# The second expert table's tiles loaded two at a time into neighbouring buffers

## The reference

```python
idx, gates                      # 8 heads x 16 picks per token, out of 128 x 128 experts
pre = einsum('tkd,td->tk', expert_u[idx], x)
act = gelu(pre) * gates
out = einsum('tk,tkd->td', act, expert_v[idx])
```

## Time and profile before

| | us |
|---|---|
| median of 3 runs | 2081.62 |
| lowest, highest run | 2081.34, 2082.43 |
| the profiled execution's own time | 2077.09 |
| its span | 2075.2 |

### The profile page before, as it was taken

One profiled execution on the slowest core, in us unless ns is written; L12 is line 12 of the kernel. 1 busy time (PEld: TensorE's weight loads), 2 busy tenths in 40 slices (PEclk: granted clock), 3 DMA queues, 4 the chain that ended last, 5 costly groups with the idle time before them and its releaser, 6 DMA issues.

```text
span 2075.2 us, 38095 instructions
## 1 busy us (share of the span) xinstructions
PE 2031.3 (98%) x12186; PEld 1857.8 (90%) x12186; DVE 1631.0 (79%) x2517; ACT 1092.8 (53%) x1460; POOL 719.6 (35%) x422
## 2 busy tenths in 40 slices
PE   7999999989999999999999999999999999999997
PEld 6888778988789999999999999999999899999876
DVE  7885777974667888888888656989898888888856
ACT  6543566454435745545554544555555555555554
POOL 0030200000001878888788860233232323334000
PEclk9999999999999999999999999999999999999999
DMA  5755558225555887788788877899999889999554
GB/s 207 257 182 182 173 172 296 110 92 193 192 173 178 212 210 206 209 209 207 210 208 207 218 243 245 319 353 357 340 360 335 297 309 324 369 339 334 201 185 150
DMA packets 172084, 496.14 MB, mean 239 GB/s; under 512 B 48720, under 2 KB 49008, under 8 KB 170352
## 3 DMA queue, kind: packets, MB, share of 16 engines
q1 hardware_dynamic: 117344, 413.39, 58.9%
q0 software_dynamic: 51200, 67.25, 12.6%
q10 hardware_dynamic: 3472, 14.72, 1.9%
HBM read 476.24 MB, written 19.04 MB: 239 GB/s over the span
## 4 chain that ended last, share of the span: by engine, by line
PE 90%; DVE 5%; DMA 2%; DVEq 1%; ACT 1%; issue 1%; ACTq 0%; SPq 0%
PE ps L263 27%; PE ps L2046 19%; PE ps L268 15%; PE ps L2051 10%; PE ps L289 5%; PE ps L283 5%; PE ps L284 5%; DVE lo L243 1%; DMA raw<-in_expert_v 1%; DVE act_pair L369 1%; PE ps L1914 1%; PE ps L1924 1%; DMA raw<-in_w_in_cols 0%; ACT hi L237 0%; PE ps L2012 0%
## 5 line engine op out<-in xcount | busy, mean ns | idle before, releaser
L237 ACT ACTIVATE hi<-raw 128x1024 fp32r<-128x1024 f32 x724 | 768.0, 1061 | 853.9 <-PE ps L263 385.1
L243 DVE TENSOR_TENSOR lo<-raw,hi 128x1024 fp32r<-128x1024 f32 x724 | 890.3, 1233 | 346.1 <-ACT hi L237 316.3
L1721 POOL DMA_INDIRECT gate_map<-gate_in_sb x256 | 471.2, 1841 | 537.7 <-DVEq L1473 462.1
L263 PE MATMUL ps<-act_pair,hi 128*128 128x448 f32 (+1 forms) x2816 | 656.6, 375 | 0.8 <-DVE act_pair L369 0.7
L263 PEld LDWEIGHTS ps<-act_pair,hi 128*128 128x128 f32 x2816 | 504.5, 189 | 53.3 <-DVE act_pair L369 3.4
L268 PEld LDWEIGHTS ps<-act_pair,lo 128*128 128x128 f32 x2816 | 371.8, 191 | 19.9 <-DVE lo L243 5.0
L268 PE MATMUL ps<-act_pair,lo 128*128 128x224 f32 (+1 forms) x2816 | 375.5, 276 | 2.6 <-DVE lo L243 2.6
L2046 PE MATMUL ps<-stage,hi 128*128 128x448 f32 x1024 | 231.9, 367 | 1.9 <-DVE gate_in_sb L1575 0.8
L2046 PE MATMUL ps<-act_pair,hi 128*128 128x448 f32 x1024 | 229.6, 366 | 1.1 <-ACT hi L237 1.1
L1738 POOL DMA_INDIRECT arena<-in_u_table,few_pick x64 | 103.0, 1610 | 305.7 <-DVE keep L1523 268.9
L2046 PEld LDWEIGHTS ps<-stage,hi 128*128 128x128 f32 x1024 | 183.1, 189 | 16.4 <-DVE gate_in_sb L1575 2.3
(11 more groups left out here) (287 smaller groups left out, 1663.6 us busy)
## 6 DMA issues: line engine op xcount, KB each, us to landing
raw<-in_expert_u SPq DMA_DIRECT2D x256, 512.0 KB
raw<-in_expert_v SPq DMA_DIRECT2D x256, 512.0 KB
raw<-in_w_in_cols SPq DMA_DIRECT2D x64, 512.0 KB
raw<-in_w_in_rows SPq DMA_DIRECT2D x48, 512.0 KB
raw<-in_w_out SPq DMA_DIRECT2D x32, 512.0 KB
raw<-in_w_pq SPq DMA_DIRECT2D x32, 512.0 KB
raw<-in_w_gate SPq DMA_DIRECT2D x32, 512.0 KB
gate_map<-stage SPq DMA_DIRECT2D x1, 14336.0 KB, 41.2
```

Of the source, the lines that this page charges most:

```text
L237: act.activation(hi[:, use, :], raw[:, slot, :], ACT.Copy).then_inc(hi_ready, 1)
L243: dve.tensor_tensor(lo[:, use, :], raw[:, slot, :], hi[:, use, :].bitcast(F32), ALU.subtract).then_inc(lo_ready, 1)
L263: mm = pe.matmul(first_tokens(out_ap), hi[:, use, d8 * P:(d8 + 1) * P], first_tokens(act_pair[:, d, :]), start=(d == 0), stop=False)
L1721: pool.indirect_dma_start(gate_map, bass.IndirectOffsetOnAxis(ap=place[0:n, unit, r:r + 1], axis=0), gates_out[0:n, unit, r:r + 1], None, ...
```

## The change

The table's layout in HBM is changed on the host: two chunks that follow each other lie side by side in a row, so that a pair of tiles is 128 rows of 8 KB. `value_block` issues two DMAs of 1 MB in place of four of 512 KB, each into two neighbouring buffers of `raw`. The wait before each is that for the pair's second tile: tile n - 3 subtracted, n being the pair's first. The completion is counted on the semaphore of the even slot alone. ScalarE's `round_tile` waits for that semaphore for both tiles of a pair; for the tiles behind the stage, `tile_at` takes off the 64 turns that the odd slots' semaphores have not counted. Rounding, subtraction, multiplication and their order are unchanged.

```diff
--- before.py
+++ after.py
@@ -229,8 +229,8 @@
                 sp.wait_ge(lo_ready, n - RAW + 1)
             sp.dma_start(raw[:, slot, :], src).then_inc(weights_landed[slot], 16)
 
-        def round_tile(act, n, slot, use, turn, first=False):
-            act.wait_ge(weights_landed[slot], 16 * turn + 16)
+        def round_tile(act, n, slot, use, turn, first=False, pairs=False):
+            act.wait_ge(weights_landed[slot // 2 * 2 if pairs else slot], 16 * turn + 16)
             if not first:
                 act.wait_ge(hi_used, n - SPLIT + 1)
                 act.wait_ge(lo_ready, n - SPLIT + 1)
@@ -246,8 +246,9 @@
         def tile_at(base, i, per, k):
 
             assert base % RAW == 0 and per % RAW == 0
+            unlanded = 2 * CHUNKS // RAW if base >= T_PLE and k % 2 == 1 else 0
             return (base + k + per * i, (base + k) % RAW, (base + k) % SPLIT,
-                    (base + k) // RAW + (per // RAW) * i)
+                    (base + k) // RAW + (per // RAW) * i - unlanded)
 
 
         def pair_tile(pe, n, use, k, out_ap, turn=None, tokens=SEQ):
@@ -582,9 +583,12 @@
                              ).then_inc(map_landed[buf], 16)
 
             def value_block(j, half=0, moved=0):
-                for k in range(RAW):
+                for k in range(0, RAW, 2):
                     n, slot, _, _ = tile_at(T_V + CHUNKS * half, j, RAW, k)
-                    load_tile(sp, n, slot, expert_v[ds(CHUNKS * half + (j + moved) * RAW + k, 1)].rearrange("a p f -> (a p) f"))
+                    sp.wait_ge(lo_ready, n + 1 - RAW + 1)
+                    pair = (CHUNKS * half + k) // 2 + (j + moved) * (RAW // 2)
+                    sp.dma_start(raw[:, slot:slot + 2, :], expert_v[ds(pair, 1)].rearrange("a p (b f) -> (a p) b f", b=2)
+                                 ).then_inc(weights_landed[slot], 16)
 
             for tb in range(TB):
                 sp.wait_ge(gates_placed[tb], 16 * PK_HEADS * TOPK)
@@ -905,7 +909,7 @@
             def value_round(half, i, here, following, first=False):
                 for c in range(4):
                     v = CHUNKS * half + 4 * i + c
-                    round_tile(act, T_V + v, c % RAW, c % SPLIT, T_V // RAW + CHUNKS // RAW * half + i)
+                    round_tile(act, T_V + v, c % RAW, c % SPLIT, T_V // RAW + CHUNKS // RAW * half + i, pairs=True)
                     if first and c < 2:
                         gelu_chunk(CHUNKS - 2 + c, c)
                     if c < 4 - AHEAD:
@@ -2142,7 +2146,7 @@
         "w_out": row_tiles(a["w_out"][0]),
         "w_pq": column_tiles(a["w_pq"][0]),
         "expert_u": u.transpose(1, 2, 4, 3, 0).reshape(2 * CHUNKS, P, TILE),
-        "expert_v": a["expert_v"][0].reshape(P, CHUNKS, 2, TILE).transpose(2, 1, 0, 3).reshape(2 * CHUNKS, P, TILE),
+        "expert_v": a["expert_v"][0].reshape(P, CHUNKS // 2, 2, 2, TILE).transpose(3, 1, 0, 2, 4).reshape(CHUNKS, P, 2 * TILE),
         "u_table": a["expert_u"][0],
         "v_table": a["expert_v"][0],
         "w_gate": row_tiles(a["w_ple_gate"][0]),
```

## The result

The changed kernel takes 2141.69 us (median of 4 runs, 2139.85 to 2147.64) against 2081.48: a ratio of 1.0299, interval 1.0282 to 1.0317. That is 60 us slower; forecast was 2147, with 2081 to 2200 as the range.

The account below looks back on a forecast made before the run. TensorE was taken to bound the kernel (98% busy), the DMA nearly full beside it. Landing plus turnaround over two pair times cost 41.6 us in the first half, 20.1 in the second, spilled rows 3: 65, so 2147 us, range 2081 to 2200.

Parts of the forecast that it names:

- The signs set down beforehand: In the stage 1301 to 1951 us: ScalarE waits about once a pair, `hi` waits over 40 us, stage some 715 us.
- Half the issues, 8 KB rows: On SP's queue, fewer issues and longer rows: taken as 0, at best returning 4.0 us.
- The wait: On SP's queue, a pair's first half is requested one tile time, 2.51 us, later; the second half when it was.
- The joint landing: At ScalarE, both tiles are usable only once the whole megabyte is there; 4.90 us on a free DMA.
- The landing: Issue to use of a 1 MB load: 4.90 us free, 6.21 and 6.05 us with two thirds of the traffic's delay.
- The turnaround: From a landing to the reissue of its buffers: 5.13 us in the first half, 4.74 in the second.
- The second half: Second half of the stage: 53 pairs with gathers lose 20.1 us, spilled rows 3 us more, last 11 pairs 0.
- The start of the stage, the tail: First pair goes out one tile later, covered by the loads' lead; the tail's loads wait as before: 0.
- The clock: TensorE's granted clock, 1.00 in the whole stage before, was left at 1.00.
- Hidden: Rival, chance 0.13: in the stage, traffic hides in the landing's non-transfer time, landing 4.9 us, no change, 2082 to 2085 us.
- Relieved: Rival, chance 0.03: longer rows reduce the DMA's work and TensorE regains idle time, at most 4.0 us, 2078 us.
- The queue stays full: Rival, chance 0.14: two pairs overlap in the DMA queue, landings of 7.93 us, 173 us slower, 2255 us.

Follow-up runs that it names:

- e2: Kernel before the change, 512 KB loads kept, but both tiles of a pair requested only after tile n-3 is subtracted; 2114.33 us, ratio 1.0144.
- e3: Kernel before the change, loads requested as before, but ScalarE waits for both tiles of a pair before its first; 2137.32 us, ratio 1.0270.
- e6: The changed kernel with gathers of an eighth of the bytes; 2090.95 us, ratio 1.0048 to the kernel before.
- e4: The changed kernel with VectorE reordered: gate multiplications and gathered-row operations moved out from between a pair's two subtractions; 2114.35 us, ratio 1.0174.
- e9: The changed kernel with both gathers of an eighth of the bytes and VectorE's shortened turnaround order; 2077.79 us, ratio 0.9999 to the kernel before.
- e5: The kernel before the change with gathers of an eighth of the bytes; 2075.50 us, ratio 0.9974.

## Why the prediction came out

**Right by mechanism, near by size, and the nearness is in part luck.** 65 us were forecast, 60 measured (62.8 in the spans). The wait, the joint landing and the cycle did what was forecast; but three terms of the sum were mis-sized, and their errors nearly cancel. The signs set down beforehand mostly came: ScalarE waited for the DMA 105 times for 128 pairs, TensorE's waits for `hi` rose to 39.1 us (over 40 was said), the stage grew by 62.8 us. Step by step:

*Half the issues, 8 KB rows: 0.* For the time, right. But this is not "nothing on the DMA": see the last section.

*The wait, 2.51 us later for the first half.* Shown by e2: alone 31 us. *The joint landing.* Shown by e3: alone 54 us.

*The landing.* The free load of the earlier trace rows, 4.90 us, was the right base: e6's chain has 4.6 to 5.0. With the traffic I took two thirds of it, 6.21 and 6.05 us. On the chain of half 0 the median was 5.47 us, so the share was nearer to a third there; behind half 0 it was 6.83 us, a little over my upper bound of 6.63 (only landings that are on the chain are counted, 29 and 19, so the long ones weigh more). The two thirds were a choice without a row, and mis-sized in both halves, in opposite directions.

*The turnaround.* 5.13 us for half 0 was too short, by a step that can be named: "Gates lie between the tiles of every second pair" was taken as a mean of 0.5 a pair. But the pairs use two sets of buffers by turns, and every block of four tiles has its gates in its first pair, so that the gates are always in the same one of the two cycles. This cycle sets the pace, and it holds all of the 1.00 us: 3.89 + 1.00 + 0.57 + 0.17 = 5.63 us, and 6.2 where a gathered row's operation comes as well; the turn shown above has 6.1. Landing too long by 0.7 and turnaround too short by 0.5 nearly cancel: 41.6 us forecast for half 0, 36.7 measured. That is luck. e4 bears out that this turnaround counts: with the gates, and the gathered rows' operations too, out of it, half 0 loses 12.5 us.

*The second half.* 20.1 and 3 us were forecast; 26.1 measured (12.4 and 13.7). "The last 11 pairs have no gathers" was wrong as to place: by the code's positions tiles 138 to 146 and 252 to 255 have none behind them, and the five pairs from tile 128 on do have some. The total of 53 pairs with second gathers stands. The read of the spilled rows led to a landing of 10.99 us on the chain (issued at 1834.68), as 11.06 before; what it cost over the kernel before wasn't separated from the rest in this kernel. In e9, where little else is lost, it is at most 2.8 us, near the 3 forecast.

*The start of the stage, the tail: 0.* The first pairs show in no difference ahead of 1301 us, and behind the stage spans differ by nothing.

*The clock: left at 1.00, and this was wrong behind half 0.* Before, the granted clock was 1.00 in the whole stage. In the changed kernel it fell to 0.50, the lower of its two levels (1.2 GHz), three times, at about 1660, 1809 and 1847 us, each time behind a stop of TensorE (3.3, 2.1 and 3.1 us long; one of 2.6 us, before 1838.62, had no fall behind it). One of them, in the changed kernel's timeline and windows:

```profile
1808.74 2.56 PE L2050 MATMUL ps<-act_pair,hi 128*128 128x448 f32 x8 [2.08 <-ACT hi L237]
1811.10 1.88 PE L2055 MATMUL ps<-act_pair,lo 128*128 128x224 f32 x8
1812.78 1.96 PE L2050 MATMUL ps<-act_pair,hi 128*128 128x448 f32 x8
...
1817.10 1.05 PE L2055 MATMUL ps<-stage,lo 128*128 128x224 f32 x8
1817.98 1.79 PE L2050 MATMUL ps<-stage,hi 128*128 128x448 f32 x8
```

```profile
1810.00:1813.00 3.00, 3.00 (x13) 2.87 (x12) 2.81 (x4) 0.12 (x1) 0.00 (x0) 0.50 0.88 309
1815.00:1820.00 5.00, 5.00 (x34) 4.76 (x33) 4.72 (x6) 3.28 (x7) 0.29 (x1) 1.00 0.56 192
```

The eight `lo` products took 1.88 us where they take 1.05, the `hi` products 2.56 and 1.96 where they take 1.79: 1.8 us on top of the wait. With the other two falls (1.1 and 1.7 us, summed in the same way) it is an estimate of 4.6 us, all behind half 0, where 26.1 us were measured against 23.1 forecast.

**Against the rivals.** *Hidden* needed a landing of 4.9 us: the narrow gathers gave this and most of the loss went (e6), and most of the rest with the shorter turnaround (e9). It is the right rival in a kernel with a quiet DMA, and the gathers decided against it. *Relieved* falls: the DMA's share did go down, and TensorE's idle time went up. By the Trainium skill, "DMA: Bandwidth & Descriptors", Rules for kernel authors, 1 MB per transfer serves the highest bandwidth; e5 and e6 bear out that the engines have less to do (shares of 0.80 and 0.71, last section), but bandwidth was not what this stage lacked. The same table of the Trainium skill also says to issue a DMA early and to wait on it late. The change did the reverse in both points: e2 and e3 show the price of each. *The queue stays full* falls for the changed kernel (5.5 us, not 7.9), as was argued: the previous pair has all but landed when the next is issued (in one case, the one of 1338.22 landed at 1343.67, and the next was issued at 1343.04). In e3, where loads do overlap in the queue, landings of this length are there (a median of 7.1 us on the chain), at no faster pace than the changed kernel's; in e4 they come with a fuller DMA. That a landing changes with pace and order is what my estimates for e2, e3 and e4 left out, and the clock besides.

**By the Trainium skill's price.** "DMA: Bandwidth & Descriptors", Anatomy of one DMA, gave an estimate of 4.4 us a landing and 36 us in all. The Trainium skill gives this fit for DMAs issued from GpSimd, which the prediction does not say; these loads are issued from SP. The measured landing with narrow gathers, 4.6 to 5.0 us, is longer than that, and the row of the trace was the better base.

## What to carry to other kernels

Merging two loads without adding buffers takes away lead twice: the first half is asked for later, and it is usable later. Before doing it, add the landing of the merged load, under the traffic of that stage, to the time from its use to the release of its buffers, and compare it with the time that the other buffers last; if it doesn't fit, the difference is paid turn after turn, though the DMA's share falls (here from 0.94 to 0.84). Then look at what else the consuming engine does between the first use and the release, by which of the alternating buffers it falls on, and not by the average. And where TensorE begins to wait, read the granted clock in narrow windows: the mean of a long one (0.97 here) hides falls to 0.50.

## What the runs showed of the hardware

**Longer rows lowered the DMA engines' share beside narrow gathers.** e5 (rows of 4 KB) and e6 (rows of 8 KB) differ in the change alone and ran on the same chip. The window of half 0, first e5, then e6:

```profile
1301.00:1626.00 325.00, 323.94 (x2049) 306.95 (x2049) 290.67 (x414) 185.21 (x258) 97.42 (x59) 1.00 0.80 261
```

```profile
1301.00:1626.00 325.00, 319.59 (x1997) 298.87 (x1997) 279.82 (x397) 167.42 (x251) 83.89 (x58) 1.00 0.71 254
```

0.80 at 261 GB/s against 0.71 at 254: 326 and 358 GB/s at a full share. e9, at 260 GB/s, has 0.71 too, but it can't be compared with e5: in a stretch that the edits leave alone it also has the lower share, with the same bytes moved. First e5, then e6, then e9:

```profile
650.00:900.00 250.00, 250.00 (x1592) 237.55 (x1591) 207.27 (x438) 143.56 (x171) 196.07 (x109) 1.00 0.81 206
```

```profile
650.00:900.00 250.00, 250.00 (x1590) 237.43 (x1589) 207.30 (x437) 143.13 (x170) 195.47 (x108) 1.00 0.80 206
```

```profile
650.00:900.00 250.00, 250.00 (x1591) 237.55 (x1591) 208.04 (x439) 143.94 (x172) 197.07 (x109) 1.00 0.74 206
```

With full gathers the gap all but vanishes: 0.94 at 344 GB/s before, 0.84 at 310 after, 366 and 369 GB/s at a full share. So the difference rests on one pair of profiles. That the rows of 8 KB aren't cut to 4 KB on the way, the page's count of packets shows: that of the queues of SP and ScalarE fell from 117344 to 98912, by 18432, which is the 16384 rows saved and 16 for each of the 128 loads saved.

**Landing time goes with the load of the DMA, but not with it alone.** Median landings of 1 MB pairs were 4.8 us at 260 GB/s (e9, half 0), 5.5 at 316 and a share of 0.85 (the changed kernel, 1320 to 1580 us), 6.2 at 337 and 0.91 (e4, the same window): 1.4 us more for the same load. (The medians are over the whole stage, the shares of the named stretch.) Against it stands e3: at a share of 0.86 and 309 GB/s in that window its half as large loads had a median of 7.1 us on the chain, with others ahead of them in the queue.

**TensorE's clock falls behind its own waits.** Counted in windows of 1 us, the granted clock was below 1 for 17 us of the stage in the changed kernel, 37 us in e3 and 29 in e2, down to 0.50; in the kernel before for none. The shares that were missing sum to 6.8, 15.3 and 12.0 us. What TensorE lost by it is less, since it was idle for a part of that time, but it counts toward the upward misses of e2 and e3.
